# Gated delta rule: a head pair's output steps handed out between the next pair's scan steps, the sums of squares of queries and keys taken later, and the last third of the last pair's output finished beside the output product

## The chip, the cores and the metric

One core of a Trainium2 chip runs the whole kernel. The metric is the device time of one execution in microseconds (us), median of three runs. All arithmetic is float32; the large products are made of three passes over operands that are split into a rounded part and its remainder.

## The reference, cut to what matters

The reference is a transformer block with product-key retrieval, followed by a block of two layers, and the change touches both layers of the second block. The first is a gated delta rule over 9 chunks of 64 positions (528 positions, the first 48 are padding), with 16 value heads that are treated as 8 pairs:

```python
def step(state, xs):                                   # one chunk
    u_c, w_c, q_c, k_c, attn_c, last_c = xs
    v_new = u_c - w_c @ state
    o = q_c @ state + attn_c @ v_new
    state = state * last_c + k_c.T @ v_new
    return state, o
...
qkv = silu(causal_conv(h @ w_in)); q, k = l2_norm(q), l2_norm(k)
o = rms_norm(o, w_norm) * silu(z)
h = h + o @ w_out
h = h + square(relu(rms_norm(h) @ w_up)) @ w_down
```

Before the scan each chunk's triangular system (I + A) is inverted. The second layer is an mLSTM with 4 pairs of heads whose output is also normalised, gated and multiplied by an output matrix.

## The kernel before

Every engine runs its own instruction list, but all lists are cut from one order written at build time: `do(kind, ...)` appends a step, and each engine then emits its part of every step in that order, with semaphore waits between engines. An instruction that waits holds up everything behind it on its engine. A stage is a set of Python generators that `merge` (L230) interleaves: each stream has a weight, and the stream with the smallest share done goes next. A stream that yields 0 can't go on yet; the others go on without it.

The delta layer runs in rounds t = 0 to 9 (L1510). In round t up to three streams are merged:

- `dense_gdn(t)`: four weight slabs of pair t (query, key, two of values, 16 steps each), two slabs of pair t - 2 for the gate z (32 steps), and the output product of pair t - 3 (32 steps). A step of the slabs is three matmuls of 256 or 272 columns. A slab's columns go through a convolution on VectorE, SiLU on ScalarE and, for query and key, squares, a sum over partitions by a matmul with ones (`sums_now`), the inverse root (`rms_inv`: Ln, then Exp, on ScalarE) and a scaling (`l2_scale`). `after(k, f)` says how many dense steps later each of these is issued. At the third slab the stream waits until one of three value buffers is free: `while not VD.can(): yield 0` (L1330). They are held by pairs t - 1, t - 2 and t - 3, and pair t - 3 gives its buffer back at the end of `out_gdn(t - 3)`. The z slabs wait for `ZG`, a single buffer, in the same way, and the output product waits for `out_ready`.
- `levels_gdn(t - 1)`: 37 steps that make the decays, the pair products and the inverse of the triangular matrix in levels 0 to 5 (`level_x`, `level_t`, three groups of chunks each).
- `scans(t)` (L1504): first all of `out_gdn(t - 3)`, then `scan_gdn(t - 2)`. `out_gdn` has for each third g (three chunks) a sum (`sums_now`), `inverse(g)` (Ln and Exp on ScalarE, then `times_z`: two multiplications on GpSimd), `gate(g)` (two multiplications on VectorE), and at the end `gdn_split` for two heads (a rounding copy on ScalarE and a subtraction on VectorE). `scan_gdn` has for each chunk c the steps `scan_r` (from the second chunk on), `scan_v`, `scan_s`: 26 in all.

PSUM banks are taken in turn: dense products use banks 0 to 2 (`PD`), everything else the five banks 3 to 7 (`PA`). A bank that held a sum is free once its Ln has been read on ScalarE. GpSimd also issues the DMAs `rows_in` and `beta_in`, each behind what stands before it on that engine.

After round 9 the last pair's last third is summed, inverted, gated and split, and then `last_outputs` (L1139) makes the output product of the last pair in two halves of the columns. The first half (272 columns) needs only the first two thirds. It also takes the sums of squares for the next norm (`sums_part`, two column blocks behind) and prepares weight slabs of the next product (`prepare(1)`: a rounding copy on ScalarE, a subtraction on VectorE). The mLSTM layer ends in the same way (L1761 to L1771).

Of the kernel before, what the change touches and what calls it, by code (L numbers as in the profile page):

```python
# [331 lines left out]
def build(nc, X, out, scratch, scratch2, scratch3):  # L332
    ctx = ExitStack()
    with ctx:
# [30 lines left out]
        def do(kind, *args):  # L365
            ORDER.append((kind, args))
# [153 lines left out]
        def sums_now(key):  # L520

            PA.take(key)
            PA.give(key, ("ln",) + key)
            do("rms_total", key)
# [611 lines left out]

        FFH, FFL, FTR, LAST_DOWN, ROOM = {}, {}, {}, {}, {}

        def last_outputs(layer, names, xs, signal, ring):  # L1139


            ws = [slab(*n) for n in names]
            key = f"ffn{layer}"
            oh, ol = xs
            sums_begin(key, HALVES, PA)
            behind = []
            for hf, (a, b) in enumerate(HALVES):
                for fb in range(8):
                    g = group(PD, [(w, fb) for w in ws],
                              lambda e, a=a, b=b: (oh[:, e, a:b], ol[:, e, a:b]), b - a,  # L1150
                              lambda e, hf=hf: ((signal, names[0][1] // 2, e, hf),))
                    dense_now(g)
                    do("resid", g, fb, a, b)
                    given_back(g, "resid", g)
                    behind.append((a, fb, "resid", g))
                    if len(behind) > 2:
                        sums_part(key, *behind.pop(0))
                    if hf and fb == 1:
                        sums_end(key, HALVES[:1])
                    if hf and fb > 2:  # L1160
                        for k in ((fb - 3) * 2, (fb - 3) * 2 + 1):
                            if k < 8:
                                norm_block(key, *HALVES[0], k, ring=ring)
                    if not hf and fb % 2 or hf and fb == 0:
                        prepare(1)
            for x in behind:
                sums_part(key, *x)
            for s in ws:
                done_with(s, g)
# [38 lines left out]
        OX = Ring([alloc2("og", 2, 528)])  # L1208
# [71 lines left out]
        def dense_gdn(t):  # L1280


            later = []

            def step():
                for x in later:
                    x[0] -= 1
                while later and later[0][0] <= 0:
                    later.pop(0)[1]()

            def after(k, f):
                later.append([k, f])
                later.sort(key=lambda x: x[0])

            def l2_squares(p, n):
                do("conv_qk", p, n)
                RT.take((p, n))
                for hf, (a, b) in enumerate(HALVES):
                    squares_ahead(("l2", p, n, hf), RT.at[p, n][:, a:b], RT.before[p, n], YC.at[p, n][:, a:b], 1.0,
                                  ("silu", p, n))  # L1300

            def l2_scale(p, n):
                (QS, KS)[n].take(p)
                do("l2", p, n)
                YC.give((p, n), ("qk", p, n, 1))
                RT.give((p, n), ("qk", p, n, 1))

            def convolve(p, n, tap):
                if tap == 3:
                    YC.take((p, n))  # L1310
                do("conv", p, n, tap)
                if tap == 0:
                    XC.give((p, n), ("conv", p, n, 0))

            def silu_v(p, n):
                do("conv_v", p, n)
                YC.give((p, n), ("vd", p, n, 1))

            for p, ns in ((t, (0, 1, 2, 3)), (t - 2, (4, 5))):
                if not 0 <= p < 8:  # L1320
                    continue
                if p == t - 2:
                    while p < 7 and not ZG.can():
                        yield 0
                    if p < 7:
                        ZG.take(p)
                for n in ns:
                    s = slab("w_gdn", 6 * p + n)
                    if n == 2:
                        while not VD.can():  # L1330
                            yield 0
                        VD.take(p)
                    for hf, (a, b) in enumerate(HALVES):
                        g = PJ[p, n, hf] = group(PD, by_slab(s), of_x(a, b), b - a, lambda k, a=a: xa(a, k))
                        for _ in dense(g):
                            step()
                            yield 1
                        if n < 4 and not hf:
                            XC.take((p, n))
                        do("gdn_take", p, n, hf)  # L1340
                        given_back(g, "gdn_in", p, n, hf)
                        if hf and n < 4:
                            for tap in range(4):
                                after(4 - tap, lambda p=p, n=n, tap=tap: convolve(p, n, tap))
                            if n < 2:
                                after(8, lambda p=p, n=n: l2_squares(p, n))
                                after(12, lambda p=p, n=n: [sums_now(("l2", p, n, hf)) for hf in range(2)])
                                after(14, lambda p=p, n=n: [do("rms_inv", ("l2", p, n, hf)) for hf in range(2)])
                                after(16, lambda p=p, n=n: l2_scale(p, n))
                            else:  # L1350
                                after(8, lambda p=p, n=n: silu_v(p, n))
                        step()
                        yield 1
                    done_with(s, g)
            p = t - 3
            if 0 <= p < 7:
                while p not in out_ready:
                    yield 0
                ws = [slab("gdn_out", 2 * p + e) for e in range(2)]
                oh, ol = OX.at[p]  # L1360
                for fb in range(8):
                    for a, b in HALVES:
                        g = group(PD, [(w, fb) for w in ws],
                                  lambda e, a=a, b=b: (oh[:, e, a:b], ol[:, e, a:b]), b - a,
                                  lambda e, p=p: (("ogl", p, e),))
                        for _ in dense(g):
                            step()
                            yield 1
                        do("resid", g, fb, a, b)
                        given_back(g, "resid", g)  # L1370
                        step()
                        yield 1
                for s in ws:
                    done_with(s, g)
                OX.give(p, ("dense", g))
            for _, f in later:
                f()
# [48 lines left out]
        def out_gdn(p):  # L1426
# [6 lines left out]
                RO.give(("out", p, g), ("og", p, g, 1))  # L1433

            sums_now(("out", p, 0))
            sums_now(("out", p, 1))
            inverse(0)
            inverse(1)
            yield 2
            sums_now(("out", p, 2))  # L1440
            inverse(2)
            yield 1
            gate(0)
            yield 1
            gate(1)
            yield 1
# [55 lines left out]
            KE.give(p, ("sn", p, 7, 1))  # L1502

        def scans(t):  # L1504
            if 0 <= t - 3 < 7:
                yield from out_gdn(t - 3)
            if 0 <= t - 2 < 8:
                yield from scan_gdn(t - 2)

        for t in range(10):  # L1510
            streams = [(dense_gdn(t), 64 * (t < 8) + 32 * (2 <= t < 10) + 32 * (t > 2))]
# [2 lines left out]
            if 0 <= t - 1 < 8:  # L1514
                streams.append((levels_gdn(t - 1), 37))
            if t > 1:
                streams.append((scans(t), 8 * (t > 2) + 26 * (t < 10)))
            merge(*streams)
        sums_now(("out", 7, 2))
        do("rms_inv", ("out", 7, 2))  # L1520
        do("times_z", ("out", 7, 2))
        do("gdn_gate", 7, 2)
        for e in range(2):
            do("gdn_split", 7, e, 1)
        room_at = gdn_end - 7 * 1152
        ROOM[0] = room_at, more_room(("up0", "down0"), 1, 3, (("so", 7, 8), ("vnm", 7, 8), ("sn", 7, 7, 1)), room_at)
        last_outputs(0, [("gdn_out", 14), ("gdn_out", 15)], OX.at[7], "ogl", XQ7)
        ffn(0)


# [229 lines left out]
            merge(*streams)  # L1760
        divided(3, 2)  # L1761
        ml_squares(3, 2)
        sums_now(("mout", 3, 2))
        do("rms_inv", ("mout", 3, 2))
        do("times_z", ("mout", 3, 2))
        do("ml_gate", 3, 2)
        for e in range(2):
            do("ml_split", 3, e, 1)
        room_at = base + 19072
        ROOM[1] = room_at, more_room(("up1", "down1"), 1, 3, (("mo", 3, 8), ("msn", 3, 7), ("mnum", 3, 2)), room_at)  # L1770
        last_outputs(1, [("ml_out", 6), ("ml_out", 7)], OX1.at[3], "mogl", XQ3)  # L1771
        ffn(1)
        do("store")

# [1516 lines left out]
```

How the kernel before makes its waits and increments, by code:

```python
    def wait_ge(self, name, *key):  # L85
        if self.q is None:
            return
        v = self.signals.value[name, key]
        sem = SHARED.get(name, name)
        if v > self.seen.get(sem, 0):
            self.q.wait_ge(self.signals.sem(sem), v)
            self.seen[sem] = v
# [121 lines left out]
def clear(engine, ring, key):  # L214
    for signal in ring.before[key]:
        engine.wait_ge(*signal)
    return ring.at[key]
# [1581 lines left out]
            def fence(i):  # L1800
                pe.drain().then_inc("fence_pe", i)
                for e in ENGINES[1:]:
                    pe.wait_ge("fence_" + e, i)
# [1 line left out]
            def constants():  # L1805
                pe.wait_ge("const", 2)
                pe.wait_ge("ones", 1)
# [1 line left out]
            def dense(g, k):  # L1809
                G = GROUPS[g]
                if k == 0:
                    clear(pe, G.ring, ("g", g))
                out = PS[G.ring.at["g", g]][:, 0:G.width]
                n, ko = G.weights[k]
                s, (hi, lo) = SLABS[n], WS.at[n]
                pe.wait_ge("w_lo_" + s.lo, n, ko // s.parts * s.parts)
                for signal in G.needs(k):
                    pe.wait_ge(*signal)
                xh, xl = G.x(k)
                last = k == len(G.weights) - 1
                pe.mm(out, hi[:, ko, :], xh, k == 0, False)
                pe.mm(out, hi[:, ko, :], xl, False, False)
                i = pe.mm(out, lo[:, ko, :], xh, False, last)
                if last:
                    i.then_inc("dense", g)
# [848 lines left out]
            def meta_in():  # L2674
                ac.wait_ge("meta", 0)
```

## Time and profile before

| | |
|---|---|
| median of 3 runs | 4079.37 us (4078.41 to 4082.83) |
| profiled execution: its time, its span | 4081.27 us, 4079.4 us |
| TensorE matmul busy | 3731.7 us, 91% |
| VectorE, ScalarE, GpSimd busy | 2611.0 us (64%), 1528.4 us (37%), 789.7 us (19%) |
| delta layer, rounds 0 to 9 | about 2030 to 2933 us of the span |
| last outputs, first layer and second layer | about 2931 to 2962 us, 3658 to 3696 us |

In the tables of the trace PE is TensorE's matmuls, PEld its weight loads, DVE VectorE, ACT ScalarE, POOL GpSimd. The profile lists which instruction ended an engine's idle time. An engine of high busy share can still lose time: the column PEclk is the clock that TensorE was granted, as a share of 2.4 GHz; at 0.50 it runs at 1.2 GHz and the same matmuls take about twice as long.

### The profile page before, as it was taken

How to read it: one execution, taken by the hardware profiler on the slowest of the kernel's cores; microseconds unless marked ns; L12 is line 12 of the kernel's file. 1: busy time of each engine (PE TensorE's matmuls, PEld its weight loads, DVE VectorE, ACT ScalarE, POOL GpSimd, SP SyncE). 2: the span in 40 equal slices, each digit the busy share in tenths (PEclk: the TensorE clock that was granted, in tenths of full speed). 3: DMA queues.
4: the chain of work that ended last, by engine and by line, in shares of the span. 5: the costliest groups of instructions: out<-in, count | busy, mean ns of one | idle time of the engine just before them, and what ended most of it. 6: DMA issues, size and time to landing. Idle time of an engine off the chain costs nothing. (4 is left out here: it accounts for less than half of the span.)

```text
span 4079.4 us, 60622 instructions
## 1 busy us (share of the span) xinstructions
PE 3731.7 (91%) x24575; PEld 3461.5 (85%) x24575; DVE 2611.0 (64%) x5091; ACT 1528.4 (37%) x2724; POOL 789.7 (19%) x661
## 2 busy tenths in 40 slices
PE   7999989989987999999889989898899999989999
PEld 5667768879987999999678888888799999978999
DVE  4664336889977999999757667676552433555342
ACT  4555323335543333333343333332341424444231
POOL 0000003556752333233131121221000001110000
PEclk9999999999998999999879999999999999989999
DMA  3122223447877999999442323332122211212221
GB/s 115 54 65 68 86 69 119 136 140 240 278 252 271 332 324 332 324 322 340 145 59 53 59 51 59 55 60 42 52 89 89 94 53 52 63 47 86 86 94 62
DMA packets 208150, 542.33 MB, mean 133 GB/s; under 512 B 18664, under 2 KB 92904, under 8 KB 207872
## 3 DMA queue, kind: packets, MB, share of 16 engines
q1 hardware_dynamic: 99792, 341.22, 24.7%
q0 software_dynamic: 42048, 150.49, 13.4%
q10 hardware_dynamic: 66032, 46.75, 3.7%
q8 instruction: 195, 3.19, 0.3%
q14 instruction: 83, 0.68, 0.1%
HBM read 492.14 MB, written 46.25 MB: 132 GB/s over the span
## 5 line engine op out<-in xcount | busy, mean ns | idle before, releaser
L95 PE MATMUL bank<-Xh,wh 128*128 128x272 f32 (+3 forms) x3680 | 1234.1, 335 | 35.3 <-DVE Xl L122 16.4
L95 PE MATMUL bank<-Xl,wh 128*128 128x272 f32 (+3 forms) x3680 | 1164.3, 316 | 0.0
L95 PE MATMUL bank<-Xh,wl 128*128 128x272 f32 (+3 forms) x3680 | 1162.7, 316 | 0.0
L122 DVE TENSOR_TENSOR wl<-raw,wh 128x1024 fp32r<-128x1024 f32 (+1 forms) x536 | 581.0, 1102 | 467.1 <-ACT wh L116 465.7
L116 ACT ACTIVATE wh<-raw 128x1024 fp32r<-128x1024 f32 (+1 forms) x632 | 589.1, 953 | 685.9 <-PE bank L95 639.8
L95 PEld LDWEIGHTS bank<-Xh,wh 128*128 128x128 f32 x3680 | 711.1, 193 | 102.6 <-issue 55.7
L95 PEld LDWEIGHTS bank<-Xl,wh 128*128 128x128 f32 x3680 | 711.7, 193 | 18.8 <-issue 2.1
L95 PEld LDWEIGHTS bank<-Xh,wl 128*128 128x128 f32 x3680 | 708.7, 193 | 20.9
L122 DVE TENSOR_TENSOR H<-H,bank 128x384 f32<-128x384 f32 (+3 forms) x522 | 250.3, 488 | 325.1 <-PE bank L95 322.1
L95 PE MATMUL bank<-aah,wh 128*128 128x384 f32 x1024 | 356.3, 348 | 43.5 <-DVE wl L122 23.6
L122 POOL TENSOR_TENSOR wl<-raw,wh 128x1024 fp32r<-128x1024 f32 x96 | 272.0, 2835 | 518.6 <-ACT wh L116 518.4
L95 PE MATMUL bank<-aal,wh 128*128 128x384 f32 x1024 | 350.0, 342 | 0.0
L95 PE MATMUL bank<-aah,wl 128*128 128x384 f32 x1024 | 349.4, 341 | 0.0
L95 PE MATMUL bank<-fh,wh 128*128 128x256 f32 (+1 forms) x1024 | 291.7, 285 | 0.0
L95 PE MATMUL bank<-fl,wh 128*128 128x256 f32 (+1 forms) x1024 | 289.1, 282 | 0.0
L95 PE MATMUL bank<-fh,wl 128*128 128x256 f32 (+1 forms) x1024 | 288.9, 282 | 0.0
L95 PEld LDWEIGHTS bank<-aah,wh 128*128 128x128 f32 x1024 | 197.9, 193 | 54.3 <-issue 29.1
L95 PEld LDWEIGHTS bank<-aal,wh 128*128 128x128 f32 x1024 | 199.7, 195 | 1.5 <-issue 1.5
L172 POOL DMA_INDIRECT row<-in_v_rows,idx x128 | 143.0, 1117 | 286.3 <-DVE acc L132 248.6
L95 PEld LDWEIGHTS bank<-aah,wl 128*128 128x128 f32 x1024 | 197.7, 193 | 0.0
L172 POOL DMA_INDIRECT row<-in_u_rows,idx x128 | 143.3, 1119 | 271.3 <-DVE row L168 225.8
L95 PEld LDWEIGHTS bank<-fh,wh 128*128 128x128 f32 x1024 | 192.6, 188 | 0.5
(314 smaller groups left out, 6191.4 us busy)
## 6 DMA issues: line engine op xcount, KB each, us to landing
raw<-in_u SPq DMA_DIRECT2D x128, 512.0 KB
raw<-in_v SPq DMA_DIRECT2D x128, 512.0 KB
raw<-in_up SPq DMA_DIRECT2D x64, 512.0 KB, 3.7
raw<-in_down SPq DMA_DIRECT2D x64, 512.0 KB, 3.4
scratch<-gb ACTq DMA_DIRECT2D x12, 2048.0 KB, 13.5
gj<-scratch SPq DMA_DIRECT2D x32, 768.0 KB
raw<-in_w_gdn SPq DMA_DIRECT2D x48, 512.0 KB
raw<-in_w_att SPq DMA_DIRECT2D x36, 512.0 KB
```

The lines of the kernel that those rows point to most:

```text
L95: return Issued(self, self.q and self.q.matmul(out, l, r, start=start, stop=stop), 1)
L116: return Issued(self, self.q.activation(out, in_, func, **kw), 1)
L122: return Issued(self, self.q and self.q.tensor_tensor(out, a, b, op), 1)
L172: return Issued(self, self.q and self.q.indirect_dma_start(out, None, in_, bass.IndirectOffsetOnAxis(ap=rows, axis=0)), 16)
```

## The change

`scans(t)` no longer runs `out_gdn` ahead of the scan: after every scan step from the second on it takes one step of `out_gdn`. The output steps are cut finer (one sum and one inverse to a step, eight steps that end in a buffer given back at the ninth call). The weight of the stream is 26 instead of 34. The sums, inverse roots and scalings of query and key come 16, 17 and 19 dense steps behind their slab instead of 12, 14 and 16. In both layers the last pair's last third becomes a generator from which `last_outputs` takes a step behind every column block, and the four slabs prepared in the first half come at column blocks 4, 5, 6, 7 instead of 1, 3, 5, 7.

```diff
-        def last_outputs(layer, names, xs, signal, ring):
+        def last_outputs(layer, names, xs, signal, ring, chain):
...
                     behind.append((a, fb, "resid", g))
+                    next(chain, None)
                     if len(behind) > 2:
                         sums_part(key, *behind.pop(0))
...
-                    if not hf and fb % 2 or hf and fb == 0:
+                    if not hf and fb > 3 or hf and fb == 0:
                         prepare(1)
...
                                 after(8, lambda p=p, n=n: l2_squares(p, n))
-                                after(12, lambda p=p, n=n: [sums_now(("l2", p, n, hf)) for hf in range(2)])
-                                after(14, lambda p=p, n=n: [do("rms_inv", ("l2", p, n, hf)) for hf in range(2)])
-                                after(16, lambda p=p, n=n: l2_scale(p, n))
+                                after(16, lambda p=p, n=n: [sums_now(("l2", p, n, hf)) for hf in range(2)])
+                                after(17, lambda p=p, n=n: [do("rms_inv", ("l2", p, n, hf)) for hf in range(2)])
+                                after(19, lambda p=p, n=n: l2_scale(p, n))
...
             sums_now(("out", p, 0))
+            inverse(0)
+            yield 1
             sums_now(("out", p, 1))
-            inverse(0)
             inverse(1)
-            yield 2
+            yield 1
+            gate(0)
+            yield 1
             sums_now(("out", p, 2))
             inverse(2)
-            yield 1
-            gate(0)
             yield 1
             gate(1)
             yield 1
...
         def scans(t):
-            if 0 <= t - 3 < 7:
-                yield from out_gdn(t - 3)
-            if 0 <= t - 2 < 8:
-                yield from scan_gdn(t - 2)
+
+            outs = out_gdn(t - 3) if 0 <= t - 3 < 7 else iter(())
+            for n, k in enumerate(scan_gdn(t - 2)):
+                yield k
+                if n > 0:
+                    next(outs, None)
...
-                streams.append((scans(t), 8 * (t > 2) + 26 * (t < 10)))
+                streams.append((scans(t), 26))
             merge(*streams)
-        sums_now(("out", 7, 2))
-        do("rms_inv", ("out", 7, 2))
-        do("times_z", ("out", 7, 2))
-        do("gdn_gate", 7, 2)
-        for e in range(2):
-            do("gdn_split", 7, e, 1)
+
+        def last_third():
+            sums_now(("out", 7, 2))
+            do("rms_inv", ("out", 7, 2))
+            do("times_z", ("out", 7, 2))
+            yield
+            yield
+            do("gdn_gate", 7, 2)
+            for e in range(2):
+                do("gdn_split", 7, e, 1)
+            yield
+
...
-        last_outputs(0, [("gdn_out", 14), ("gdn_out", 15)], OX.at[7], "ogl", XQ7)
+        last_outputs(0, [("gdn_out", 14), ("gdn_out", 15)], OX.at[7], "ogl", XQ7, last_third())
...
         divided(3, 2)
         ml_squares(3, 2)
-        sums_now(("mout", 3, 2))
-        do("rms_inv", ("mout", 3, 2))
-        do("times_z", ("mout", 3, 2))
-        do("ml_gate", 3, 2)
-        for e in range(2):
-            do("ml_split", 3, e, 1)
+
+        def last_third1():
+            yield
+            sums_now(("mout", 3, 2))
+            do("rms_inv", ("mout", 3, 2))
+            do("times_z", ("mout", 3, 2))
+            yield
+            yield
+            do("ml_gate", 3, 2)
+            for e in range(2):
+                do("ml_split", 3, e, 1)
+            yield
+
...
-        last_outputs(1, [("ml_out", 6), ("ml_out", 7)], OX1.at[3], "mogl", XQ3)
+        last_outputs(1, [("ml_out", 6), ("ml_out", 7)], OX1.at[3], "mogl", XQ3, last_third1())
```

## Rows read from the trace of the kernel before

**Rows 1.** The page: TensorE's busy tenths in 40 slices of the span.

```profile
PE   7999989989987999999889989898899999989999
```

**Rows 2.** Waits of TensorE, 2160 to 2950 us: total us, times, longest.

```profile
PE bank L95 <- ACT rt L116: 22.0, 5, 4.9
PE bank L98 <- ACT ro L116: 20.5, 6, 5.5
PE bank L95 <- DVE ta L162: 18.5, 6, 7.8
```

**Rows 3.** Busy time by round: length, PE, PEld, DVE, ACT, POOL, then PEclk, DMA share, GB/s.

```profile
2256.60:2362.60 106.00, 96.29 (x757) 89.44 (x756) 73.24 (x149) 38.68 (x82) 20.32 (x27) 0.97 0.29 52
...
2685.50:2792.40 106.90, 97.61 (x757) 90.82 (x756) 74.78 (x152) 39.47 (x83) 21.24 (x27) 0.95 0.31 57
2792.40:2883.00 90.60, 77.19 (x597) 69.86 (x596) 60.97 (x128) 26.15 (x54) 16.19 (x20) 0.92 0.18 40
```

**Rows 4.** Timeline of TensorE, round 4: start, duration, idle before and its releaser.

```profile
2371.30 0.90 PE L98 MATMUL bank<-cst,vd 128*128 128x128 f32 x3 [3.20 <-ACT ro L116]
...
2385.84 0.91 PE L95 MATMUL bank<-ta,bb 128*128 128x128 f32 x6 [2.38 <-DVE ta L162]
...
2392.37 2.10 PE L95 MATMUL bank<-rt,ones 128*128 128x272 f32 x4 [4.92 <-ACT rt L116]
```

**Rows 5.** Busy time in stretches of 10 us around round 4, columns as in rows 3.

```profile
2340.00:2350.00 10.00, 10.00 (x87) 9.49 (x86) 7.59 (x19) 2.39 (x6) 0.00 (x0) 1.00 0.37 79
...
2370.00:2380.00 10.00, 8.70 (x60) 8.09 (x60) 8.05 (x12) 5.97 (x13) 7.92 (x11) 0.83 0.32 57
...
2390.00:2400.00 10.00, 7.63 (x38) 7.25 (x39) 6.33 (x14) 7.04 (x15) 0.00 (x0) 0.66 0.07 29
```

**Rows 6.** Timeline of VectorE, start of round 4.

```profile
2374.86 3.31 DVE L132 SCALAR_TENSOR_TENSOR dd<-dd,cc,cst 128x128 f32<-128x128 f32 x3
...
2381.61 0.81 DVE L122 TENSOR_TENSOR bb<-sq,bb 128x384 f32<-128x384 f32 x1 [2.22 <-DMA sq<-scratch]
...
2383.27 1.48 DVE L132 SCALAR_TENSOR_TENSOR z<-vd,cols,ro 128x192 f32<-128x192 f32 x2
```

**Rows 7.** Timeline of ScalarE, start of round 4.

```profile
2391.06 0.64 ACT L116 ACTIVATE yc<-yc 128x528 f32<-128x528 f32 x1 [9.51 <-DVE yc L132]
```

**Rows 8.** Timeline of GpSimd, start of round 4.

```profile
2371.89 2.58 POOL L122 TENSOR_TENSOR ro<-ro,z 128x192 f32<-128x192 f32 x4 [5.30 <-ACT ro L116]
```

**Rows 9.** Groups on VectorE by form, 2310 to 2360 us: busy us, mean ns, idle before.

```profile
L162 DVE STREAM_TRANSPOSE ta<-tb 128x384 f32<-128x384 f32 x9 | 5.2, 579 | 0.3
L122 DVE TENSOR_TENSOR xr<-bank,cst 128x384 f32<-128x384 f32 x9 | 5.0, 555 | 6.0 <-PE bank L95 6.0
L122 DVE TENSOR_TENSOR tb<-tb,bank 128x192 f32<-128x192 f32 x11 | 3.9, 354 | 5.2 <-PE bank L95 5.2
L132 DVE SCALAR_TENSOR_TENSOR st<-st,lb,bank 128x128 f32<-128x128 f32 x12 | 3.6, 342 | 3.3 <-PE bank L95 3.3
```

**Rows 10.** Timeline of TensorE, round 8 and the start of round 9.

```profile
2801.00 0.90 PE L98 MATMUL bank<-cst,vd 128*128 128x128 f32 x3 [5.47 <-ACT ro L116]
...
2814.91 3.20 PE L95 MATMUL bank<-ta,bb 128*128 128x128 f32 x12 [7.81 <-DVE ta L162]
...
2887.99 0.46 PE L95 MATMUL bank<-dd,vn 128*128 128x128 f32 x2 [2.79 <-ACT vn L116]
```

**Rows 11.** Timeline of TensorE, round 0.

```profile
2068.68 2.10 PE L95 MATMUL bank<-rt,ones 128*128 128x272 f32 x4 [6.01 <-ACT rt L116]
```

**Rows 12.** Timeline of TensorE, last outputs of the first layer.

```profile
2933.52 1.08 PE L95 MATMUL bank<-ro,ones 128*128 128x384 f32 x2 [2.50 <-ACT ro L116]
...
2939.72 0.73 PE L95 MATMUL bank<-sq,ones 128*128 128x272 f32 x2 [1.50 <-ACT sq L116]
```

**Rows 13.** Timeline of TensorE, last outputs of the second layer.

```profile
3666.81 1.62 PE L95 MATMUL bank<-ro,ones 128*128 128x384 f32 x2 [8.15 <-ACT ro L116]
...
3673.64 0.70 PE L95 MATMUL bank<-sq,ones 128*128 128x272 f32 x2 [1.57 <-ACT sq L116]
```

## The prediction

> **What bounds the kernel now.** I read the page first: TensorE is busy in nine tenths or more of most slices, and the slices of the delta layer (the 21st to the 29th of forty) alternate between 8 and 9 [rows 1]. So TensorE sets the time, and what can be won lies in the idle spots and slow stretches. The waits of TensorE over rounds 2 to 8 name three: 22.0 us on squares that ScalarE writes (`rt`), 20.5 us on the inverse roots of the outputs (`ro`), 18.5 us on transposed matrices from VectorE (`ta`) [rows 2]. The 5.5 us and 7.8 us that are longest in two of them are round 8's [rows 10]; without them the five rounds 3 to 7 lose (22.0 + 15.0 + 10.7) / 5 = 9.5 us each.
>
> The timeline of round 4 shows the order, and it is the same in all five: within 25 us of a round's start TensorE stops for a bank that an output sum still holds, then for `ta`, then for the squares of the query slab [rows 4]. After 2400 us nothing is lost; a stretch late in a round is busy throughout, 87 matmuls in 10 us, 0.115 us each [rows 5]. So the loss is a jam at the start of the round. Its cause is on VectorE. It works through decays, pair products, gates and the convolution of slab 0 without a pause that TensorE causes; ScalarE has the SiLU of that slab waiting 9.5 us on it [rows 7]. Three decays take 3.31 us while GpSimd multiplies by z [rows 6, 8], and a product waits 2.22 us for the DMA of beta [rows 6], which GpSimd issues behind its four multiplications of 2.58 us [rows 8].
>
> A second loss follows the waits: the granted clock is 0.83 and 0.66 in the two stretches of 10 us that hold the first and the last wait [rows 5], so (0.17 + 0.34) x 10 = 5.1 us of full clock are missing. Over whole rounds, 0.97 in the first and 0.95 in the last of the five is 3.2 and 5.3 us [rows 3]; four at about 5.3 make a mean of 4.9. Some 0.6 of it falls into idle time, which leaves 4.3 us. A round of 3 to 7 thus loses 9.5 + 4.3 = 13.8 us.
>
> **The change in rounds 3 to 7.** I counted the steps through the merge rule for both weights.
>
> 1. The output sums. Today both first sums stand at the round's head, and their Ln waits on ScalarE behind the decays' Exp. After the change the first sum comes behind 9 dense steps and two pair steps, the others two scan steps on, with the scan's own steps between. The wait of 3.0 us (15.0 / 5) goes.
>
> 2. The `ta` wait (2.1 us). VectorE loses from before this point one gate (1.5 us), the DMA wait (2.2) and the slow decays (3.31 less three at about 0.34, by the nearest form of 128 columns [rows 9], 2.3 us), and gains one state copy and one residual of the scan, about 1 us. That is 5 us less ahead of a wait of 2.1, while TensorE arrives 3.2 us earlier for want of the first wait but has some 2.7 us of scan steps new before it. It goes.
>
> 3. The squares wait (4.4 us). VectorE's queue to the end of the convolution shrinks by about 6 us (a second gate is now behind it too). TensorE asks later by 4 dense steps (12 matmuls, 1.4 us) and about 4.5 us of scan and level steps, and earlier by the 5.6 us of the two other waits. So it asks about 0.3 us later than now, at the old end less 4.6, when the squares have been there for 1 us. I take 0.5 us, bounds 0 and 2.5.
>
> 4. The new wait. The value buffer is given back by the ninth output step, which now falls at 10 of 26 scan steps, 38% of the round; before it was 8 of 34, 24%. But slab 2 needs it at 32 of 128 dense steps, 25%. So dense work stops there, and TensorE gets nine steps in a row without it: s2, t10, t11, r3, t12, v3, x20, x21, s3 (r, v, s with the chunk for scan steps, x, t with level and group). They have 56 matmuls, 6.4 us at 0.115. To get to x21 VectorE must do a gate (1.5), state updates (0.7), a mask (0.56), three times `tb` and `ta` (3 x 0.93) [rows 9], a residual (0.35) and two split subtractions (about 0.6 each, by the mask's row), 7.1 us. And it comes with a backlog: between the end of slab 0's convolution and this point stand 6.3 us (a key step 1.1, two gates 3.0, state 0.7, two masks 1.1, a residual 0.4), against 2.8 us that TensorE spends there (SiLU 0.64, squares about 0.8, sums 1.05, a dense step). The wait is 7.1 + 3.5 - 6.4 = 4.2 us. Bounds: 0 if the work overlaps well, and 7.8, the longest wait that a stretch without dense work shows [rows 10].
>
> 5. Then 20 dense steps come together, 6.9 us, beside which VectorE has the convolution of slab 1. Its sums are asked for about 5.5 us after the start; I take 0.7 us, bounds 0 and 3.
>
> 6. The clock. One wait of 4 us remains instead of two or three. The 3.20 us wait was followed by a shortfall of 1.7 us and the 4.92 us wait by 3.4 us [rows 4, 5]; I take 2.0, bounds 0 and 3.4.
>
> A round after: 0.5 + 4.2 + 0.7 + 2.0 = 7.4 us against 13.8, a gain of 6.4, five times: 32 us. The z slabs (at 50%) and the output product (at 75%) lie behind 38% and don't wait.
>
> There is a place where VectorE and GpSimd collide. The row is that of the three decays in 3.31 us beside GpSimd's multiplications [rows 6, 8]; in my sum that cost is gone, since `times_z` moves away from the decays. The Trainium skill (SBUF — State Buffer, "SBUF: two separate sides") says that the two engines share a pair of ports as an exclusive lock, so that a VectorE instruction with two SBUF inputs and a GpSimd one that reads SBUF block each other for a whole instruction. The trace agrees with 3.31 us against about 1.0. By that rule the cost isn't gone, it moves to whatever stands on VectorE beside `times_z` next, and the 2.3 us would come back in each of five rounds, 11 us in all.
>
> **The other places.** Round 8 has no slabs, and its z slabs wait for the single gate buffer, which the same ninth output step gives back. Before, output steps and nine level steps ran bare, with 5.47 and 7.81 us of waits [rows 10]. Now ten scan steps and fourteen level steps run bare. That adds about 8 us to VectorE's list there, of which some 4 to 5 us fill its own waits, and takes 9.6 us of work from the rest of the round, which was full. Gain 6 us, bounds 0 and 10. Round 9: the first scan step waited 2.79 us behind the splits [rows 10], with a slower clock behind it; gain 2.5, bounds 0 and 5. Round 0: the squares wait of 6.01 us [rows 11] shrinks by the four dense steps; gain 1, bounds 0 and 2.
>
> Last outputs. In the first layer the total waits 2.50 us and the first sum of squares 1.50 us [rows 12]. TensorE now makes one column block (0.7 us) before the total, but the first square stands on ScalarE behind the split's copies, as before; it only loses a slab's rounding of 1 us ahead of it. Gain 1. In the second layer TensorE waits 8.15 us for the last division and square, now with two column blocks made (1.4 us), and the gate comes a block behind the first square, so the 1.57 us wait nearly goes [rows 13]. Gain 2.5. Four slab preparations in a row give VectorE about 1.66 us per block against 1.2 on TensorE; three banks cover this. Both together 3.5, bounds -1 and 6.
>
> **The sum.** 32 + 6 + 2.5 + 1 + 3.5 = 45 us. The profiled execution has a span of 4079.4 us in a time of 4081.27, and the median is 4079.37, so span and median are the same to 0.1 us: 4079.4 - 45 = 4034 us.
>
> **Rivals.**
> - *The new wait takes most of it.* Nine steps without dense work are bound by VectorE to the full 7.8 us [rows 10] and the clock falls as behind 4.92 us: 0.5 + 7.8 + 0.7 + 3.4 = 12.4 against 13.8, 7 us in five rounds, with half of the rest (6) 13 us: 4066. For it speaks that the longest wait in the trace is just of this kind; against it that in round 8 VectorE had the pair products in that stretch, which here lie earlier.
> - *The change gives back at the start what it takes later* (no change). The jam would move as a whole. VectorE is busy 73 to 75 of 107 us in a round [rows 3], so this needs a second engine's limit; late in the round it has a quarter idle [rows 5]. Time 4079 within 8.
> - *Slower.* Place: the bare stretch at 25% of rounds 3 to 7. It pays the 7.8 us and leaves VectorE so late that slab 1's squares, asked for in one burst of dense work, cost the old 4.9 us again with the full 4.3 of clock: 17 against 13.8, 16 us more, less 6 elsewhere: 4089. It decides once waits and clock of a round exceed 15 us.
> - *Nearly all goes.* Bare stretch 1 us or less, no slow clock: a round loses 2, gains 12, 59 in all, with 15 elsewhere: 4005.
>
> **Chances and range.** Forecast (4015 to 4055) 0.62, nearly all goes 0.12, the new wait takes most 0.13, no change 0.07, slower 0.06. A measurement of this kernel tells about 0.2%, 8 us, from no change. Faster 0.62 + 0.12 + 0.13 = 0.87, same 0.07, slower 0.06. The range reaches from the best to the third case, 4005 to 4066.
>
> **What would show it.** Right: no wait on `ro` at the pair transposes; the first scan step right at a round's start; one gap of 3 to 5 us near a quarter of each round, ended by `ta` or `vn`, with level and scan matmuls alone around it; then 20 dense steps in a row; rounds of about 101 us instead of 107. Wrong: gaps of 7 us there, a wait on `rt` that stays above 3 us, or PEclk still 0.95 over a round. I would be most wrong in step 4, where a backlog on VectorE is a difference of long sums.

## The result, and the profile after

The changed kernel takes 4123.34 us (median of 4 runs, 4119.59 to 4125.38) against 4080.66 us before (4 runs): a ratio of 1.0104, 95% interval 1.0086 to 1.0121. It is 43 us **slower**, where 45 us faster was forecast. The profiled spans are 4123.5 and 4079.4 us.

The page of the changed kernel, TensorE's busy tenths and its granted clock in 40 slices. Against [rows 1] little is to be seen: in the slices of the delta layer 8 takes the place of 9 in some.

```profile
PE   7999989989988999999878888888899999989999
...
PEclk9999999989988999999979999999999999999999
```

The waits of TensorE in the changed kernel, 2160 to 2950 us (total us, times, longest), which answer to [rows 2]:

```profile
PE bank L95 <- ACT vn L116: 38.9, 10, 6.2
PE bank L95 <- DVE st L132: 19.1, 15, 2.4
PE bank L95 <- DVE rc L132: 16.1, 11, 2.1
...
PE bank L95 <- DVE ta L162: 3.5, 2, 2.8
PE bank L95 <- ACT rt L116: 0.9, 1, 0.9
```

The waits on `ro` have gone, and those on `ta` and `rt` all but (3.5 and 0.9 us are left), as forecast. Three others stand in their place: the copy `vn` on ScalarE, and two results of VectorE, the updated state `st` and the residual `rc`. The table of windows for rounds 3 to 7 as one stretch (length, PE, PEld, DVE, ACT, POOL, PEclk, DMA share, GB/s) says how much that is. Before:

```profile
2256.60:2792.37 535.77, 485.58 (x3776) 452.04 (x3775) 372.27 (x752) 196.66 (x409) 105.13 (x127) 0.96 0.30 56
```

The changed kernel, the five rounds and then round 4 alone:

```profile
2269.80:2832.48 562.68, 501.90 (x3774) 468.43 (x3773) 368.58 (x752) 196.21 (x409) 105.29 (x126) 0.92 0.28 53
...
2380.60:2494.50 113.90, 101.33 (x757) 94.61 (x756) 73.77 (x152) 39.44 (x82) 21.05 (x26) 0.91 0.29 53
```

The five rounds are 26.9 us longer with the same matmuls. The view of waits over these stretches adds up to 49.3 us before and 60.7 us after, which is 11.4 us more; the busy time of the same matmuls grew by 16.3 us, with the clock down from 0.96 to 0.92. (The two add up to a little over 26.9 us, as the view of waits and the table count idle time slightly differently.) So more of the loss is slow clock than waiting.

Over the whole span, by the starts of the rounds (GpSimd's copy `xr` of the keys) and of the first layer's feed-forward part (ScalarE's first `ft`): round 0 is 1.0 us shorter, rounds 1 and 2 are 14.2 us longer, rounds 3 to 7 26.9 us longer, and from round 8 through the last outputs 4.1 us longer. That makes 44.2 us, the whole difference of the two spans (44.1 us). The mLSTM layer and what follows give no more.

The timeline of TensorE in round 4 of the changed kernel, which answers to [rows 4]:

```profile
2389.45 0.77 PE L95 MATMUL bank<-dd,vn 128*128 128x128 f32 x2 [5.36 <-ACT vn L116]
...
2411.21 0.44 PE L95 MATMUL bank<-st,qk 128*64 128x128 f32 x4 [0.82 <-DVE st L132]
...
2421.34 0.44 PE L95 MATMUL bank<-st,qk 128*64 128x128 f32 x4 [2.01 <-DVE st L132]
...
2423.83 0.80 PE L95 MATMUL bank<-rc,tb 128*128 128x128 f32 x2 [1.24 <-DVE rc L132]
...
2446.72 0.77 PE L95 MATMUL bank<-rc,tb 128*128 128x128 f32 x2 [2.12 <-DVE rc L132]
```

Three places matter. One wait of 5.36 us stands at the very start of the round; it is a wait that the prediction doesn't have. The third and fourth lines lie in the stretch without dense work at a quarter of the round: the scan and level matmuls follow each other with no slab's matmul between. Its waits are 2.01 + 1.24 = 3.2 us against 4.2 forecast. The last line lies behind the end of the key slab; the prediction has no wait there. What follows the two waits of the stretch is in the windows of 4 us, columns as above:

```profile
2420.00:2424.00 4.00, 1.42 (x11) 1.14 (x12) 3.93 (x12) 1.18 (x2) 0.00 (x0) 0.81 0.91 78
2424.00:2428.00 4.00, 4.00 (x20) 4.00 (x20) 2.33 (x5) 0.28 (x1) 0.00 (x0) 0.50 0.34 136
2428.00:2432.00 4.00, 4.00 (x19) 3.66 (x19) 2.84 (x7) 1.56 (x2) 0.00 (x0) 0.50 0.00 0
2432.00:2436.00 4.00, 4.00 (x32) 4.00 (x32) 0.59 (x1) 1.67 (x4) 0.00 (x0) 0.91 0.00 0
```

TensorE idles for more than half of the first window (1.42 of 4.00 us busy), and then it works for 8 us and more at 0.50, its lower level of 1.2 GHz. These four windows lack (0.19 + 0.50 + 0.50 + 0.09) x 4 = 5.1 us of full clock. Windows of 1 us show where the clock fell: between the two waits, about 1 us behind the end of the first.

```profile
2421.00:2422.00 1.00, 0.66 (x7) 0.52 (x7) 0.96 (x4) 0.89 (x2) 0.00 (x0) 1.00 1.22 82
2422.00:2423.00 1.00, 0.59 (x6) 0.45 (x5) 0.97 (x4) 0.00 (x0) 0.00 (x0) 0.75 0.75 53
2423.00:2424.00 1.00, 0.17 (x1) 0.17 (x2) 1.00 (x3) 0.00 (x0) 0.00 (x0) 0.50 0.67 107
```

### The profile page after: what moved, and what is told of

Its sections match the earlier page's. It is cut to its first block and busy times, and to the rows that moved or that the text cites. A ratio compares the mean times of both kernels' runs of the same rounds, so it can differ in the third digit from the quotient of the medians.

```text
span 4123.5 us, 60643 instructions
## 1 busy us (share of the span) xinstructions
PE 3761.8 (91%) x24575; PEld 3488.7 (85%) x24575; DVE 2602.5 (63%) x5091; ACT 1529.9 (37%) x2726; POOL 787.5 (19%) x661
## 5 line engine op out<-in xcount | busy, mean ns | idle before, releaser
L95 PE MATMUL bank<-Xh,wh 128*128 128x272 f32 (+3 forms) x3680 | 1230.5, 334 | 35.1 <-DVE Xl L122 16.2
L95 PEld LDWEIGHTS bank<-Xl,wh 128*128 128x128 f32 x3680 | 715.9, 195 | 16.2 <-issue 0.6
```

Of the source, the lines that this page charges most:

```text
L95: return Issued(self, self.q and self.q.matmul(out, l, r, start=start, stop=stop), 1)
```

## The experiments

The theories at the start: *later sums* (the later sums, inverse roots and scalings of query and key cost the time), *interleaving* (the output steps between the scan steps cost it: the wait at the start, the stretch without dense work, the clock), and *last outputs* (the last thirds and the later preparations cost it).

**The parts one by one.** Three kernels take one part each of the diff on the kernel before, and a fourth hands out the output steps twice as fast in the changed kernel.

```diff
 # e1: kernel before, with
-after(12, sums_now ...)  after(14, rms_inv ...)  after(16, l2_scale ...)
+after(16, sums_now ...)  after(17, rms_inv ...)  after(19, l2_scale ...)
 # e2: kernel before, with out_gdn's new order, the new scans(t) and the weight 26
 # e3: kernel before, with last_third, last_third1 and the preparations at fb > 3
 # e4: changed kernel, with a second output step behind each scan step
                 if n > 0:
                     next(outs, None)
+                    next(outs, None)
```

Later sums alone:

> The kernel before with only the later sums, inverse roots and scalings of query and key (16, 17, 19 dense steps behind the slab). Theory A (the parts add up, and the later sums are what lengthened rounds 1 and 2 of the changed kernel by 9 and 5 us, since no output steps exist there): rounds 1 and 2 longer by about 14 us together, rounds 3 to 7 shorter by up to 2 us each because the wait on the squares shrinks, the whole 4 to 14 us slower. Theory B (rounds 1 and 2 are longer only because of what the other parts do to them): 5 to 15 us faster, from the squares waits of 4.4 us in five rounds.

Measured: 4130.3 us against 4081.66, ratio 1.0120 [1.0103, 1.0137]. This part alone costs 49 us, more than the whole change, and far more than either theory allowed (14 us slower at most).

Interleaving alone:

> The kernel before with only the output steps handed out between the scan steps (weight 26), sums of query and key as before. Theory A: rounds 3 to 7 longer by 5 us each (new wait of the first scan step on ScalarE's copy, stretch without dense work, slow clock behind both), round 8 shorter by 3, rounds 1 and 2 within 3 us of before: 25 to 35 us slower. Theory B: rounds 1 and 2 longer too, 40 us slower.

Measured: 4075.15 us, ratio 0.9989 [0.9980, 0.9999]: 6.5 us faster by the medians, 4.5 by the ratio, just clear of no difference. Both theories had it 25 us slower or more, and both are wrong. In rounds 3 to 7 of it no wait on `rt` is left, with the sums still at 12 steps: the interleaving alone takes the squares wait away, and the later sums bought nothing there.

The last thirds alone:

> The kernel before with only the last thirds as generators in the last outputs of both layers and the preparations at column blocks 4 to 7. Both theories: the end of the second layer's last outputs 1.6 us earlier, as in the changed kernel. The first layer's is what is open: Theory A 0 to 2 us gained there (3 us faster in all, the same within the measurement), the other theory (late preparations starve the products behind) 3 to 7 us lost.

Measured: 4082.59 us, ratio 1.0004 [0.9995, 1.0014]: no difference. The second layer's gain of 1.6 us can't be told in it; from round 8 through the first layer's last outputs it takes 3.0 us more than before, the lower end of what the other theory gave for late preparations.

The three parts add up: 48.6 - 6.5 + 0.9 = 43.0 us slower by the medians, where the whole change is 42.7 us slower. So nothing is left for the parts to do to each other.

Two output steps behind each scan step:

> The changed kernel, with two output steps after each scan step instead of one, so that the value buffer is given back at 6 of 26 scan steps (23%), ahead of the third slab. Theory A (the stretch without dense work costs its waits of 4.1 us and the half clock behind it, the first scan step's wait stays): rounds 3 to 7 shorter than in the changed kernel by 5 to 9 us each, 25 to 40 us faster than it, so about the time before. Rival (the jam on VectorE just comes back with the gates earlier): under 10 us faster than the changed kernel.

Measured: 4136.33 us, ratio 1.0137 [1.0120, 1.0154]: 13 us slower than the changed kernel, where 25 to 40 us faster was expected. In its rounds 3 to 7 TensorE waits 38.3 us on the state `st` (14.8 in the changed kernel), with the wait on `vn` at 26.1 us as in the changed kernel. With the later sums in place, an earlier return of the value buffer gives nothing; without them the same edit is worth 7 us (f5 below).

**What the later inverse root meets.** The timeline of ScalarE in e1, where a key slab ends:

```profile
2537.88 0.39 ACT L116 ACTIVATE xc<-bank 128x256 f32<-128x256 f32 x1 [0.25 <-PE bank L95]
2538.28 1.28 ACT L110 ACT_TABLE_LOAD   x1
2539.58 0.49 ACT L116 ACTIVATE rt<-bank,eps 128x272 f32<-128x272 f32 x1
...
2540.92 0.42 ACT L116 ACTIVATE rt<-rt 128x256 f32<-128x256 f32 x1
2541.25 1.14 ACT L116 ACTIVATE wh<-raw 128x512 fp32r<-128x512 f32 x2
```

And in the kernel before, at the same place of the round:

```profile
2501.99 1.28 ACT L110 ACT_TABLE_LOAD   x1
...
2504.63 0.42 ACT L116 ACTIVATE rt<-rt 128x256 f32<-128x256 f32 x1
...
2505.91 0.39 ACT L116 ACTIVATE xc<-bank 128x256 f32<-128x256 f32 x1
2506.19 1.14 ACT L116 ACTIVATE wh<-raw 128x512 fp32r<-128x512 f32 x2
```

A slab has 16 steps. At 14 the inverse root of one slab falls three steps ahead of the end of the next, and it is over when that slab's last copy `xc` comes; at 17 it is issued between that copy and the rounding `wh` of the weight slab that is prepared when a slab is done. The table load and two Ln and two Exp take from 2538.28 to 2541.25, so the rounding starts 3.4 us behind the start of its copy instead of 0.3. The subtraction `wl`, which needs the rounding, holds up VectorE's list. First VectorE, then TensorE in e1:

```profile
2541.89 1.29 DVE L122 TENSOR_TENSOR wl<-raw,wh 128x512 fp32r<-128x512 f32 x2 [2.56 <-ACT wh L116]
...
2545.15 0.48 DVE L139 COPY st<-bank 128x128 f32<-128x128 f32 x2
```

```profile
2545.78 0.44 PE L95 MATMUL bank<-st,qk 128*64 128x128 f32 x4 [1.99 <-DVE st L139]
```

VectorE idles 2.56 us, and the taps of the convolution, the state copy `st`, the level results `tb`, `ta` and the residual `rc` stand behind it; TensorE asks for `st` and waits 1.99 us. The Trainium skill (ScalarE: Activation LUTs, "What ACT_TABLE_LOAD costs") counts, besides the 1283 ns of the load, some 1.4 us in which the engine drains. The trace agrees with the first and not with the second: the load takes 1.28 us and the Ln starts 0.02 us behind its end.

How much it is shows in the waits of VectorE, 2040 to 2900 us, of e1 and of the kernel f3 below:

```profile
DVE wl L122 <- ACT wh L116: 52.9, 33, 3.1
```

```profile
DVE wl L122 <- ACT wh L116: 11.5, 20, 1.3
```

The kernel before has the same 11.5 us in 20 as f3. The timeline of VectorE in e1 has sixteen waits on `wh` of 1.9 to 3.1 us, 42.5 us in all, that the kernel before doesn't have: two in each of the eight rounds with slabs, one for the query's inverse root and one for the key's. In the changed kernel the row is 55.4 us in 34; 6.8 us of it are one wait in round 8 that the interleaving brings (it stands in e2 and g1 too), and the sixteen are 38.3 us.

**One step of it.** If the place in ScalarE's list is the cause, then late scaling alone must be free, and an inverse root one step later still, behind the rounding, must give the time back with the sums as late as in the change.

```diff
 # f1: kernel before, with the scaling alone later
-after(16, l2_scale ...)
+after(19, l2_scale ...)
 # f3: kernel before, with the inverse root behind the slab's end
+after(16, sums_now ...)  after(18, rms_inv ...)  after(20, l2_scale ...)
```

> The kernel before with only the scaling of query and key later (sums 12, inverse roots 14, scaling 19 dense steps behind the slab). Theory A (what costs the 48 us of the later sums is the place of the inverse root: at 17 its table load, two Ln and two Exp stand on ScalarE just ahead of the rounding of the next weight slab, and VectorE waits for that rounding with its convolution behind it): within 8 us of before. Theory B (the cost is the scaling, which at 19 falls between the taps of the next convolution on VectorE and holds them): 20 to 48 us slower.

Measured: 4083.63 us against 4080.16, ratio 1.0006 [0.9997, 1.0016]: no difference.

> The kernel before with sums at 16, inverse roots at 18 and scaling at 20 dense steps: against the first experiment one step later, so that the inverse root stands behind the rounding of the next slab on ScalarE. Theory A (place of the inverse root against the rounding): waits of VectorE for the rounded slab fall from 53 us to about 12, the time comes back to within 15 us of before. Theory B (scaling between the taps, or later sums as such): as slow as the first experiment or slower, 40 to 55 us.

Measured: 4084.9 us, ratio 1.0015 [1.0005, 1.0024]: 4.7 us slower where e1 was 49 us slower. The waits on the rounding are back at 11.5 us, as Theory A had it. The timeline of ScalarE in f3 at this place has the rounding first:

```profile
2506.53 0.39 ACT L116 ACTIVATE xc<-bank 128x256 f32<-128x256 f32 x1
2506.81 1.14 ACT L116 ACTIVATE wh<-raw 128x512 fp32r<-128x512 f32 x2
2507.97 1.28 ACT L110 ACT_TABLE_LOAD   x1
2509.26 0.49 ACT L116 ACTIVATE rt<-bank,eps 128x272 f32<-128x272 f32 x1
```

One step of the dense stream is worth 44 us. The scaling moves by that step too, from 19 to 20; f1 shows that a scaling at 19 costs nothing by itself, and a kernel with the inverse root at 18 and the scaling left at 19 wasn't run. The other direction is the changed kernel with the old distances:

```diff
 # g1: changed kernel, with
-after(16, sums_now ...)  after(17, rms_inv ...)  after(19, l2_scale ...)
+after(12, sums_now ...)  after(14, rms_inv ...)  after(16, l2_scale ...)
```

> The changed kernel with sums, inverse roots and scalings of query and key back at 12, 14 and 16. Theory A (the later sums alone lost the time; interleaving and last thirds together are worth what they were worth alone): 4070 to 4082 us, about 45 us less than the changed kernel. Theory B (interleaving and later sums only lose together): above 4090 us.

Measured: 4077.78 us against 4080.49, ratio 0.9994 [0.9984, 1.0004]. With this the slowdown is shown from both sides: put into the kernel before it costs 49 us, taken out of the changed kernel it gives 46 us back. The profiled execution of g1 was its slowest (4084.48 us). In its rounds 3 to 7 (538.33 us) the waits add up to 45.6 us against 60.7 in the changed kernel. Its timeline of TensorE in round 4, in the stretch without dense work, and the windows of 4 us behind it:

```profile
2399.29 0.44 PE L95 MATMUL bank<-st,qk 128*64 128x128 f32 x4 [0.82 <-DVE st L132]
...
2401.79 0.56 PE L95 MATMUL bank<-rc,tb 128*128 128x128 f32 x2 [1.25 <-DVE rc L132]
```

```profile
2400.00:2404.00 4.00, 2.75 (x16) 2.61 (x16) 3.47 (x9) 0.28 (x1) 0.00 (x0) 0.76 0.74 201
2404.00:2408.00 4.00, 4.00 (x29) 3.81 (x28) 2.43 (x6) 1.56 (x2) 0.00 (x0) 0.81 0.01 2
2408.00:2412.00 4.00, 3.96 (x29) 3.65 (x29) 1.18 (x2) 2.38 (x5) 0.00 (x0) 1.00 0.00 0
```

The same stretch waits 0.82 instead of 2.01 us for the state. With 1.2 us less of waiting in front, the clock stands at 0.76 and 0.81 and is then full, where the changed kernel had 0.81, 0.50, 0.50 and 0.91: 1.7 us of clock missing against 5.1. (The windows of the changed kernel begin 1.3 us ahead of the matmul that waited for the state, those of g1 0.7 us behind it; windows laid alike give the same two figures.) In the changed kernel Ln and Exp (here without a table load) take the 1.66 us from 2416.41 to 2418.07 on ScalarE between copy and rounding, `wl` on VectorE waits 1.13 us for it, and the state update that TensorE asks for stands behind; in this round that is how the late inverse root turned into slow clock. The wait of 2.12 us at 2446.72 us is gone in g1 too; ahead of it `wl` had waited 3.03 us for the key's inverse root.

**What limits the interleaving.** ScalarE in the changed kernel, start of round 4, and VectorE beside it:

```profile
2386.92 1.28 ACT L110 ACT_TABLE_LOAD   x1 [3.27 <-DVE dd L132]
2388.21 0.94 ACT L116 ACTIVATE dd<-dd 128x384 f32<-128x384 f32 x2
2389.05 0.26 ACT L116 ACTIVATE vn<-bank 128x128 f32<-128x128 f32 x1
```

```profile
2381.71 4.39 DVE L122 TENSOR_TENSOR wl<-raw,wh 128x512 fp32r<-128x512 f32 x4 [0.24 <-ACT wh L116]
2386.03 1.66 DVE L132 SCALAR_TENSOR_TENSOR dd<-dd,cc,cst 128x128 f32<-128x128 f32 x6
```

The first scan step of a round needs only the copy `vn`, 0.26 us; it stands behind the decays' Exp, that behind a table load, and all of it behind the decays on VectorE, which come after four subtractions. That is the 5.36 us wait. Four kernels try to pull this apart, each built on the last (f4 on e2):

```diff
 # f4: the scan stream merged ahead of the levels
+                streams.append((scans(t), 26))
                 if 0 <= t - 1 < 8:
                     streams.append((levels_gdn(t - 1), 37))
-                streams.append((scans(t), 26))
 # f5: f4, and a second output step behind each scan step
                     next(outs, None)
+                    next(outs, None)
 # g3: f5, and more dense work between decays and first pair product
-            yield 1
+            yield 4
...
-                    streams.append((levels_gdn(t - 1), 37))
+                    streams.append((levels_gdn(t - 1), 40))
 # g4: g3, with last_third1 in the second layer's last_outputs
```

> The interleaving alone (second experiment) with the scan's stream merged ahead of the levels' stream, so that the copy of the first scan step stands on ScalarE ahead of the decays' Exp. Theory A (the wait of 5.4 us at each round's start is that copy queued behind an Exp that waits for VectorE): that wait goes, and with it the half clock behind it, rounds 3 to 8 shorter by 4 to 8 us each, 4030 to 4050 us. Rival (the wait only moves to the pair products, which need the same decays a few steps on): under 10 us faster than the second experiment.

Measured: 4070.86 us against 4080.16, ratio 0.9980 [0.9970, 0.9990], 4.3 us less than the second experiment: the rival's case. The scan step no longer waits, the next product of the levels does (timeline of TensorE, f4):

```profile
2374.22 1.65 PE L95 MATMUL bank<-qk,xr 128*128 128x128 f32 x6 [4.80 <-DVE dd L122]
```

> As the kernel before it in this list, with two output steps after each scan step, so that the value buffer is back at 23% of the round and dense work never stops. Theory A: the waits of 2 to 3 us in the stretch without dense work go too, 3 to 6 us less in each of rounds 3 to 7: 4010 to 4035 us. Rival (gates and inverse roots come back into the jam of the pair products): equal to or slower than one step at a time.

Measured: 4064.07 us, ratio 0.9963 [0.9950, 0.9975]: the fastest kernel of the study, 16 us faster than before (its rounds 3 to 7 are 16.2 us shorter than before), but 29 us short of Theory A's 4035. Rounds 3 to 7 shrink from f4 to f5 by 9.8 us. The waits in them add up to 38.0 us in f4 and 38.2 us in f5; the row of windows of f4, and then that of f5, shows that the busy time of the same matmuls fell instead, with the clock up from 0.93 to 0.96. Why the same sum of waits goes with a higher clock in f5 isn't shown:

```profile
2258.34:2787.71 529.37, 491.19 (x3774) 460.24 (x3773) 356.70 (x752) 195.29 (x409) 102.58 (x127) 0.93 0.29 56
```

```profile
2254.69:2774.27 519.58, 481.38 (x3774) 450.54 (x3773) 359.61 (x752) 194.66 (x409) 101.38 (x125) 0.96 0.31 58
```

> The fastest kernel so far (interleaving, two output steps to a scan step, scan's stream first), with three more units between the decays and the first pair product in the levels' stream (weight 40), so that TensorE has some ten dense steps more while VectorE makes the decays. Theory A (the 4.8 us wait of the second pair product on the decays is a matter of order): it falls to 1 us or so, with the slow clock behind it; 4 to 7 us less in each of seven rounds, 4020 to 4045 us. Rival (VectorE's total up to that point sets it, the wait comes back a few steps later): within 8 us of 4064.

Measured: 4072.02 us against 4080.49, ratio 0.9977 [0.9966, 0.9988], 8 us slower than f5. The wait on the decays was split and not shortened: in rounds 3 to 7 it is 23.4 us in 5 in f5 and 32.0 us in 10 in g3. Those rounds are 2.6 us longer in g3; the rest was lost elsewhere. Waits of TensorE in g3, 2160 to 2950 us; `dd` was 32.3 us in 8 and `vn` 6.7 us in 4 in f5:

```profile
PE bank L95 <- DVE dd L122: 40.7, 13, 4.6
PE bank L95 <- ACT vn L116: 17.1, 9, 5.5
```

> As the kernel before it in this list, with the last third of the second layer as a generator in its last outputs as well (nothing changed in the first layer's, preparations as before). If the last third in the second layer is worth the 1.6 to 2 us that the traces of the changed kernel and of the third experiment show there: 1 to 3 us less than the kernel before it in this list, which a few runs can hardly tell; the trace should show the layer's last outputs shorter by 2 us.

Measured: 4074.07 us, ratio 0.9984 [0.9975, 0.9994]; the second layer's part adds nothing to g3, where 1 to 3 us less was expected. That agrees with e3.

## Why the prediction was wrong

The runs show *later sums*: e1 has the whole loss, g1 and f3 give it back. The interleaving by itself was right in its sign and far too large in its size. So two steps failed: step 3 turned the sign and accounts for 46 us of the 89 us between forecast and measurement (4123.34 against 4077.78 for g1), and a wait at the round's start that the sum put at nothing took most of the rest, the gain of the interleaving.

1. **Step 1 and step 2 (`ro`, `ta`): the waits went, as forecast.** No wait on `ro` is left in rounds 3 to 7 of the changed kernel, and the two on `ta` outside them are 3.5 us. But step 2 also took 2.3 us of slow decays a round off VectorE's list, because `times_z` moves away from them. That did not happen. Beside the last three decays of round 4 there is again a `times_z` in the changed kernel (VectorE, then GpSimd):

```profile
2397.34 2.87 DVE L132 SCALAR_TENSOR_TENSOR dd<-dd,cc,cst 128x128 f32<-128x128 f32 x3
```

```profile
2397.94 1.17 POOL L122 TENSOR_TENSOR ro<-ro,z 128x192 f32<-128x192 f32 x2
```

All decays of rounds 3 to 7 take 23.8 us in it and took 24.1 before. (In e2 they take 20.3 us, so it hangs on where each multiplication falls.) What those 2.3 us a round were worth in time, no run shows.

2. **Step 3 is the step that failed.** It treated the later sums as 4 dense steps of grace for the squares and priced only that wait. The wait did go (in e1 from 22.0 to 3.0 us over rounds 3 to 7). But the inverse root is a step on ScalarE too, and the prediction never asked what it is moved past: at 17 it stands ahead of the rounding of the next weight slab, behind which VectorE's list stands. Price: 1.9 to 3.1 us of VectorE twice a round, which in e1 makes the waits of rounds 3 to 7 67.8 us instead of 49.3 and the clock 0.94 instead of 0.96, 33 us in all. The rest of e1's loss lies in rounds 1 and 2 (16 us), which the prediction had unchanged.
3. **Step 4 (the stretch without dense work): right in place and kind, 3.2 us against 4.2.** Without the later inverse root it is 2.1 us (g1). The releasers are `st` and `rc`, on VectorE as foreseen, where `vn` or `ta` had been named.
4. **The first scan step of a round is the second failure: a wait that the sum put at nothing**, 5.4 us in round 4, 26.0 us over rounds 3 to 7. I had it "right at a round's start" and didn't look at what stands ahead of its copy on ScalarE. It took back about all that steps 1 and 2 gave (15.1 + 10.7 us). In f4 it became a wait of 4.8 us on the decays; g3, with more work between, only split it. That supports VectorE's work at the round's start as what sets it, but doesn't show it: a kernel with less of that work wasn't run.
5. **Step 6 (clock): 2.0 us a round forecast.** At 0.91 round 4 lacks 0.09 x 113.9 = 10 us; before, at 0.95, it was about 5. By windows, 3.4 us of the 10 lie at the wait of the round's start, 5.1 behind the stretch without dense work and 1.7 behind the 2.12 us wait at the key slab's end. Only the second has a place in the prediction.
6. **Step 5 held**: no wait on the squares of slab 1 shows in rounds 3 to 7.
7. **The other places gave nothing.** From round 8 through the first layer's last outputs 6 + 2.5 + 1 = 9.5 us were to be gained; measured are 4.1 us lost in the changed kernel, 0.8 lost in e2 and 3.0 lost in e3. In the first layer a new wait of 2.04 us on a prepared slab and one of 2.68 us on a square took the place of the old 2.50 and 1.50; both new ones stand in e3 as well (1.73 and 2.69 us), so they come with the last thirds and the late preparations. In the second layer the two waits of [rows 13], 8.15 + 1.57 = 9.7 us, became five: 0.66 on the split, 1.68 on a prepared slab, 2.83 on the last third, 0.37 and 2.27 on squares, 7.8 us in the changed kernel and 9.6 in e3. Kernels that leave this layer as it was take 729.9 to 733.7 us from one feed-forward part to the next, those that change it 731.4 to 734.3, so no gain can be told. Behind that, the second feed-forward part takes 376.3 to 376.4 us in the four kernels with the late preparations (changed kernel, e3, e4, g1) and 374.9 to 375.0 us in the nine others: about 1.5 us lost, with the same matmuls and the same waits, and 0.97 instead of 1.00 of clock in its first 55 us. The other differences of 2 us in these places are not explained.

The rivals: "slower" came true in sign, but for another reason and in another size (its jam was to be at the squares of slab 1, and its time 4089 us). Without the later sums the time is nearest to "the change gives back at the start what it takes later" (4079 within 8): g1 has 4078 us and e2 4075, and the wait on `vn` at the round's start (26.0 us in e2) stands in place of the waits on `ro` and `ta` (25.8). "The new wait takes most of it" had 4066 us, but by 7.8 us in the stretch without dense work, which no kernel shows there. "Nearly all goes" is what no kernel came near.

## What to carry to other kernels

- When a step is moved in an order that all engines share, list for every engine that it touches what it now stands ahead of, not only whether its own consumer still gets it in time. A piece of 3 us, twice a round on an engine that is busy for 37% of the time, cost 49 us, since the rounding behind it held up VectorE's whole list; one step further on it cost 5 us.
- A delay counted in steps should be read against the period of what repeats (here 16 steps to a slab): 14 is a harmless place and 18 nearly one (5 us), 17 is the slab's end.
- Try the parts of a change one by one: the good part here (16 us in f5, with two more edits) was hidden under a part that had been thought harmless.

## What the runs showed of the hardware

- Small waits close together can be followed by much slower clock. In round 4 of the changed kernel waits of 2.01 and 1.24 us stand within 4.5 us; the granted clock fell from full to 0.50, TensorE's lower level, between the two and stayed there for more than 8 us. In g1, with 0.82 and 1.25 us at the same place, it fell behind the second and was full again some 3 to 4 us later. The prediction had priced the clock by the length of a single wait.
- VectorE's instructions get slower beside GpSimd's. At the start of round 4 four subtractions `wl` of 512 columns, beside GpSimd's two multiplications `qe`, take 4.39 us in the changed kernel, 1.1 us each, and 4.50 us in the kernel before; two take 1.29 us elsewhere (0.64 each). Three decays beside `times_z` take 3.31 us before and 2.87 us in the changed kernel, while six without it take 1.66 (0.28 each). The line of the kernel before:

```profile
2363.24 4.50 DVE L122 TENSOR_TENSOR wl<-raw,wh 128x512 fp32r<-128x512 f32 x4 [0.24 <-ACT wh L116]
```

The Trainium skill (SBUF — State Buffer, "SBUF: two separate sides") states that the two engines take a shared pair of ports as an exclusive lock, for a whole instruction. The trace agrees with 4.39 us against 2.6, and with the time of the decays, which did not go away with the change.
